# The two MLPs' down projections in another order: P6 with the middle products, P3 and P4 last, tile by tile

## The reference

```python
def sqrelu_mlp(x, w_up, w_down):
    return jnp.square(jax.nn.relu(x @ w_up)) @ w_down     # 1024 -> 4096 -> 1024

x = layer_norm(ALPHA * x + mix, ...)                      # attention, projected
x = layer_norm(ALPHA * x + sqrelu_mlp(x, mlp_w_up[layer], mlp_w_down[layer]), ...)
```

## Time and profile before

| | |
|---|---|
| time, median of 3 runs | 1939.84 us (1938.89 to 1945.38) |
| the profiled execution's own time | 1945.18 us |
| its span (first to last instruction) | 1943.4 us |
| PE busy | 1842.1 us (95%), 9436 matmuls |
| DVE busy | 1393.8 us (72%) |
| ACT busy | 882.3 us (45%) |
| POOL busy | 803.1 us (41%) |
| DMA | 297.86 MB, mean 153 GB/s |
| mean granted clock of PE | 0.979 |

### The profile page before, as it was taken

One profiled execution on the slowest core, in us unless ns is written; L12 is line 12 of the kernel. 1 busy time (PEld: TensorE's weight loads), 2 busy tenths in 40 slices (PEclk: granted clock), 3 DMA queues, 4 the chain that ended last, 5 costly groups with the idle time before them and its releaser, 6 DMA issues.

```text
span 1943.4 us, 25413 instructions
## 1 busy us (share of the span) xinstructions
PE 1842.1 (95%) x9436; PEld 1497.2 (77%) x9436; DVE 1393.8 (72%) x2217; ACT 882.3 (45%) x1512; POOL 803.1 (41%) x570
## 2 busy tenths in 40 slices
PE   9999899999999899999999999897999999999997
PEld 7877578777778788766877777677887888888876
DVE  4568857878898842275787888975559788776766
ACT  4247643444355432384343435465554554343442
POOL 1234533544451100182344444304446457777740
PEclk9999899999999899999999999898999999999999
DMA  7321033888866423203288886551211323333344
GB/s 282 109 91 45 1 141 97 318 295 288 293 234 197 151 87 108 88 2 98 96 316 282 293 291 246 178 174 45 87 66 47 128 84 112 109 109 130 109 152 152
DMA packets 66536, 297.86 MB, mean 153 GB/s; under 512 B 8496, under 2 KB 8816, under 8 KB 46064
## 3 DMA queue, kind: packets, MB, share of 16 engines
q1 hardware_dynamic: 59360, 254.45, 37.8%
q0 software_dynamic: 7056, 41.80, 5.9%
HBM read 258.54 MB, written 35.65 MB: 151 GB/s over the span
## 4 chain that ended last, share of the span: by engine, by line
PE 65%; DVE 21%; DMA 5%; ACT 3%; issue 3%; POOL 2%; SPq 0%; POOLq 0%; ACTq 0%; DVEq 0%
PE G L458 29%; PE G L2838 5%; PE G L2904 4%; PE TR L2904 4%; PE OB L2904 3%; DVE og_sb L3393 3%; DMA KS_sb<-ada 3%; DVE weights_low L666 2%; PE TR L458 2%; PE OB L458 2%; PE G L1906 2%; PE G L2857 2%; POOL weights_low L502 1%; PE TR L2838 1%; PE OB L1906 1%
## 5 line engine op out<-in xcount | busy, mean ns | idle before, releaser
L458 PE MATMUL G<-xt_high,weights_high 128*128 128x512 f32 (+1 forms) x1224 | 451.7, 369 | 0.7 <-DVE xt_low L1526 0.4
L458 PE MATMUL G<-xt_low,weights_high 128*128 128x512 f32 (+1 forms) x1224 | 449.7, 367 | 0.0
L458 PE MATMUL G<-xt_high,weights_low 128*128 128x512 f32 (+1 forms) x1224 | 449.5, 367 | 0.0
L502 POOL TENSOR_TENSOR weights_low<-ring_sb,weights_high 128x1024 fp32r<-128x1024 f32 (+2 forms) x102 | 244.4, 2408 | 300.4 <-ACT weights_high L496 300.4
L496 ACT ACTIVATE weights_high<-ring_sb 128x1024 fp32r<-128x1024 f32 (+2 forms) x188 | 189.6, 1019 | 158.4 <-DMA ring_sb<-chunks 43.6
L458 PEld LDWEIGHTS G<-xt_high,weights_high 128*128 128x128 f32 x1224 | 229.1, 187 | 41.0 <-issue 1.9
L458 PEld LDWEIGHTS G<-xt_high,weights_low 128*128 128x128 f32 x1224 | 228.9, 187 | 38.5
L458 PEld LDWEIGHTS G<-xt_low,weights_high 128*128 128x128 f32 x1224 | 228.9, 187 | 38.0
L666 DVE TENSOR_TENSOR weights_low<-ring_sb,weights_high 128x1024 fp32r<-128x1024 f32 (+1 forms) x160 | 200.8, 1258 | 78.6 <-ACT weights_high L659 78.2
L502 DVE TENSOR_TENSOR weights_low<-ring_sb,weights_high 128x1024 fp32r<-128x1024 f32 (+1 forms) x86 | 109.5, 1283 | 170.0 <-ACT weights_high L496 169.9
L659 ACT ACTIVATE weights_high<-ring_sb 128x1024 fp32r<-128x1024 f32 (+1 forms) x160 | 158.0, 989 | 117.9 <-PE G L2904 68.0
(11 more groups left out here) (637 smaller groups left out, 4288.8 us busy)
## 6 DMA issues: line engine op xcount, KB each, us to landing
ring_sb<-chunks SPq DMA_DIRECT2D x91, 1024.0 KB, 4.8
ring_sb<-ups SPq DMA_DIRECT2D x64, 512.0 KB, 4.1
KS_sb<-ada SPq DMA_DIRECT2D x64, 512.0 KB, 4.6
ring_sb<-down_sums SPq DMA_DIRECT2D x64, 512.0 KB, 3.9
ring_sb<-downs SPq DMA_DIRECT2D x16, 1024.0 KB, 6.9
down_sums<-ring_sb POOLq DMA_DIRECT2D x16, 1024.0 KB, 6.0
rows_sb<-downs SPq DMA_DIRECT2D x14, 1024.0 KB, 7.3
down_sums<-rows_sb POOLq DMA_DIRECT2D x14, 1024.0 KB, 5.9
```

The costliest lines, as they stand in the source:

```text
L458: mm = nc.tensor.matmul(out, lhsT=a, rhs=b, start=(3 * i + j == 0), stop=(3 * i + j == n - 1))
L502: tt_(out=quarter_part(wl, stage, n), in0=quarter_part(raw_quarter(stage, n), stage, n), in1=quarter_part(wh, stage, n), op=ALU.subtract). ...
```

## The change

The number of products, matmuls and split columns is the same. Their order and the engine of some of them differ.

- `LINEAR`: D14 now follows U31, D13 lies between U30 and U31, then B0, D15, B1 to B3. P6 leaves the last phase and becomes "S" (6 matmuls), interleaved with B from unit 3 on. The last phase is "C": P3 and P4 from one tile (12 matmuls per unit).
- `SPLITS`: ACT, DVE and SP follow their own list, which has C0 and C1 ahead of S15.
- `NORMAL` = 8 (first MLP) or 10 (second): from this unit on all C weights are held, and PE passes P3 tile 0, P3 tile 1, P4 tile 0, P4 tile 1, with a tile of the next stage transposed behind a pass.
- The buffer `KS4` now holds raw D14, not D15. B has three raw buffers instead of four, S two in XT.
- The modulation uses two buffers, `og` and `w2`; its PE sums stand one or two up products later; its part 1 ends behind D14.
- The low parts of C's staged hidden blocks (512 columns per unit) are made by POOL (`last_low`), no longer by DVE.
- In the second MLP POOL's `gpsimd_inputs` comes after all hidden sums, `scale_columns` behind C3, and the context's norm is cut in two, behind B8 and B11.

```diff
+    for u in range(11):
+        LINEAR += [("D", u), ("U", 6 + 2 * u), ("U", 7 + 2 * u)]
+    LINEAR += [("D", 11), ("U", 28), ("U", 29), ("D", 12), ("U", 30), ("D", 13), ("U", 31), ("D", 14), ("B", 0), ("D", 15)]
+    LINEAR += [("B", 1), ("B", 2), ("B", 3), ("S", 0)] + [x for u in range(4, 15) for x in (("B", u), ("S", u - 3))]
+    LINEAR += [("S", 12), ("B", 15), ("S", 13), ("S", 14), ("S", 15)] + [("C", u) for u in range(UNITS)]
-    ADA_SUM_BEHIND = {5: 0, 8: 1, 11: 2, 15: 3, 20: 4, 23: 5, 26: 6, 29: 7}
+    ADA_SUM_BEHIND = {7: 0, 10: 1, 13: 2, 16: 3, 21: 4, 25: 5, 28: 6, 31: 7}
+        ADA_SUM = [ogf, w2[:, :, :, :].rearrange("p a b c -> p (a b c)")]
...
         def raw_down(u):
-            return flat(KS4[:, :, :]) if u == UNITS - 1 else flat(rows[:, :, :]) if u % 2 else ring[:, 1, 2048:4096]
+            return flat(KS4[:, :, :]) if u == 14 else flat(rows[:, :, :]) if u % 2 and u < 15 else ring[:, 1, 2048:4096]
...
-                    elif u == UNITS - 1:
+                    elif u == 14:
                         sp.wait_ge(ada_steps, 64 * (i + 1))
+                    elif u == 15:
+                        sp.wait_ge(sums_stored[0], down_count(stage, 12))
...
+                def last_low(u):
+                    gp.wait_ge(staged_h, staged_at(stage, "C", u))
+                    tt(out=unit_r(u)[:, 1:3, :], in0=unit(u)[:, 1:3, :], in1=unit_r(u)[:, 0::3, :], op=ALU.subtract).then_inc(last_l, 1)
...
                 if stage == "mlp1":
-                    gpsimd_inputs(gp)
                 gain()
                 for u in range(UNITS):
-                    gp.wait_ge(staged_l, staged_at(stage, "B", u))
+                    gp.wait_ge(staged_l, low_at(stage, "B", u))
                     tt(out=a21, in0=a11, in1=a21, op=ALU.add).then_inc(hid_last, 1)
+                    if u >= 6:
+                        last_low(u - 6)
+                for u in range(UNITS - 6, UNITS):
+                    last_low(u)
+                if stage == "mlp1":
+                    gpsimd_inputs(gp)
...
+                normal = NORMAL[stage]
+                pe.wait_ge(dve_out, v + 14)
+                third(0, (0, 1))
+                for u in range(normal):
+                    if u + 1 < normal:
+                        third(u + 1, (0, 1))
+                    if u == 0:
+                        pe.wait_ge(dve_out, v + 18)
+                    fourth(u, (0, 1)).then_inc(quarters, 1)
+                for t in range(2):
+                    for u in range(normal, UNITS):
+                        mm = third(u, (t,), u == UNITS - 1)
+                    mm.then_inc(prod_done, 1)
+                    after(t)
+                for u in range(normal, UNITS):
+                    mm = fourth(u, (0,), u == UNITS - 1)
+                mm.then_inc(prod_done, 1)
+                after(2)
+                for u in LAST_PASS[stage]:
+                    fourth(u, (1,), u == LAST_PASS[stage][-1]).then_inc(quarters, 1)
+                after(3)
...
 # DVE, in mlp():
-                        if part or j:
-                            dve.wait_ge(ada_cols, 4 * part + j)
+                        if 4 * part + j > 1:
+                            dve.wait_ge(ada_cols, 4 * part + j - 1)
...
+                # behind the splits of all C tiles
+                quarters_in(dve, stage, AT["S", 15] + 1)
+                dve.wait_ge(dve_out, v + 18)
+                for t in range(2):
+                    evacuate(2 + t, 1, P6B[t])
+                    evacuate(2 + t, 0, P6B[t])
+                    evacuate(t, 1, P6B[t])
+                early(2, 1, 19)
+                early(3, 1, 22)
```

More of the change, by code:

```diff
@@ L661, in mlp_low, with mlp_weights @@
-        def mlp_low(dve, stage, n):
-            kind, u = LINEAR[n]
-            dve.wait_ge(w_hi, SPLIT0[stage] + n + 1)
-            wh, wl = mlp_weights(kind, u)
+                eng.wait_ge(first_sums_in[u % 3], 16 * ((6, 5, 5)[u % 3] * i + u // 3 + 1))
+            elif kind == "S":
+                eng.wait_ge(sixth_sums_in[u % 2], 16 * (8 * i + u // 2 + 1))
+            else:
+                eng.wait_ge(last_sums_in[u % 4], 32 * (4 * i + u // 4 + 1))
+        def mlp_weights(stage, kind, u):
+            if kind == "S":
+                return [x[:, 3, 512 * (u % 2):512 * (u % 2) + 512] for x in (Wh, Wl)]
+            if kind == "C" and u >= NORMAL[stage]:
+                row, last = HELD_IN[stage][u]
+                if row is not None:
+                    return flat(Hh[:, row:row + 2, :]), flat(Hh[:, row + 2:row + 4, :])
+                r = C_ROWS[last % 4]
+            else:
+                r = C_ROWS[u % 4] if kind == "C" else u % 3 if kind == "B" else 3 if (kind, u) == ("D", 15) else AT[kind, u] % 4
+            return Wh[:, r, :], Wl[:, r, :]
@@ L2978, in fourth, with last_left, third @@
+                def last_left(u, k):
+                    return [unit_r(u)[:, 3 * k, :], unit_r(u)[:, 1 + k, :]]
+                def third(u, ts, last=False):
+                    ready("C", "C", u)
+                    for t in ts:
+                        mm = block(P3B[t], t, last_left(u, 1), rights("C", u, 1), u == 0, last)
+                    return mm
+                def fourth(u, ts, last=False):
+                    ready("C", "C", u)
                     for t in ts:
-                        mm = block(P4B[t], t, lefts("A", u, 0), rights("F", u, 0), u == 0, u == UNITS - 1)
+                        mm = block(P4B[t], t, last_left(u, 0), rights("C", u, 0), u == 0, last)
@@ L3474, in evacuate, with early @@
                     ins.then_inc(dve_out, 1)
+                def early(t, half, n):
+                    dve.wait_ge(dve_out, v + n)
+                    nc.vector.bn_stats(stat[:, t, half, :], X[:, t, half * 512:(half + 1) * 512]).then_inc(ln_dve, 1)
                 done = 4
@@ new lines, in mlp, with last_tile @@
+                quarters_in(dve, stage, AT["S", 15] + 1)
+                dve.wait_ge(dve_out, v + 18)
+                for t in range(2):
+                    evacuate(2 + t, 1, P6B[t])
[3 more added lines that the diff above has]
+                early(3, 1, 22)
+                def last_tile(t, half):
+                    if t < 2:
+                        dve.wait_ge(prod_done, ends + 2 + t)
+                        dve.wait_ge(dve_out, v + (21, 24)[t])
+                        evacuate(t, 1, P3B[t])
+                    else:
@@ L3757, in _ @@
             xt_low_tile("x1", 0, 3)
-            mlp("mlp0", ALPHA, 0, lambda chain: {
-                ("bi", 0): lambda: chain(0), ("bi", 1): lambda: (chain(1), xt_low_tile("x2", 8, 0)), ("s1", 2): lambda: xt_low_tile("x2", 8, 1)})
+            mlp("mlp0", ALPHA, 0, between("x2", 8, True))
             xt_low_tile("x2", 8, 2)
```

521 lines of the change are left out of this document (240 added, 281 removed).

## The result

| | before | after |
|---|---|---|
| time, median, first comparison | 1940.8 us (1938.9 to 1945.4, 4 runs) | 1924.6 us (1923.4 to 1927.8, 4 runs) |
| time, median, a later comparison | 1945.7 us (1942.9 to 1947.6, 7 runs) | 1925.7 us (1924.1 to 1926.6, 4 runs) |
| the profiled execution's own time | 1945.2 us | 1925.5 us |
| its span | 1943.4 us | 1923.7 us |
| PE busy | 1842.1 us | 1835.0 us |

The ratio after to before is 0.9916 with a 95% interval of 0.9894 to 0.9938 in the first comparison and 0.9901 (0.9884 to 0.9917) in the later one: 16 and 19 us less. The forecast was 39 less, 1901 us. The time lies inside the range of 1880 to 1932, but the gain is half of what was forecast, or less.

The account below looks back on a forecast made before the run. PE was taken as the bound, busy for 95% of the span. 73.2 us go and 33.9 come, 39.3 less than the profiled 1945.2: 1905.9, as a median 1901 us; range 1880 to 1932.

Parts of the forecast that it names:

- what goes, all terms: Both MLPs: PE's idle and slow-clock time at modulation steps, D14, POOL's back-to-back sums and the MLP ends goes, 73.2 us.
- D13 behind raw D14: Between U30 and U31: PE newly waits 3.7 us for D13's hidden block, plus 1.6 of clock, twice: 10.6 us.
- D14 again: Behind U31: D14's block is late after B0's weight split, D15 and hidden sums; 3 us, twice: 6.
- the middle phase: Interleaved B and S units: DVE needs 4.7 us a unit against PE's 4.1; 2 and 5.5 us lost, sum 7.5.
- the tail: Last phase's tile 0: P6's evacuations behind C15's split make PE idle 2.0 and 4.1 us; with clock 9.8.
- nothing is relieved: Low parts on POOL (`last_low`): no relief for DVE, which waits while POOL works; no separate size given.
- the modulation: Up products: PE's ten waits for the last modulation step, 19.4 us, go, with 8 of clock: 27.4.
- the pile: Second MLP: POOL's ten back-to-back hidden sums after `scale_columns`, stalling DVE and PE, disappear; 10.2 us with clock.
- A: Rival: both new waits at D13 and D14 are absent because modulation runs ahead with two buffers; 1884 us, chance 0.20.
- B: Rival: up products are bound by loads, late modulation weights keep the 27.4 us of waits; 1928 us, chance 0.17.
- C: Rival: DVE and POOL hand-offs bound the middle phase, units 6 to 14, at 7.8 us each; 1960 us, chance 0.10.

## Why the prediction was wrong

By its own steps. The unit is idle time plus half of the slow-clock time. In the third column a slow stretch counts at half its length even where PE idled in it, so what came adds up to 57 and not to 54.7.

| step | forecast | in the trace after |
|---|---|---|
| what goes, all terms | 73.2 | 72.8 in the trace before |
| D13 behind raw D14 | 10.6 | 9.3 idle + 5.1 |
| D14 again | 6 | 4.3 + 1.7 |
| the middle phase | 7.5 | 12.2 idle + 5.1 |
| the tail | 9.8 | 7.0 idle + 7.1 (clock, and short waits) |
| short D and C waits | none | 5.3 |

- **The step that failed is "the middle phase"**, taken as 2 and 5.5 us. It summed DVE's work per unit (4.7 against PE's 4.1) and asked by how much nine units fall behind. In the trace a unit costs DVE 3.8 in the first MLP, and PE doesn't wait in these units but for 1.6 us in the second; the loss is one wait of 5.4 and 5.2 at the end, S15's, behind two splits and four evacuations. That was readable from the diff (`SPLITS` puts C0 and C1 ahead of S15) and wasn't priced. Shown: the order of these steps by itself is worth 8.2. The term is the largest miss, 9.8 of the 23 us by which what came was over the forecast; the others are 4.3 at the tail, 3.8 at D13, and 5.3 in short waits at D and C blocks that had no term.
- **The price of POOL's low part** is the second half of it. The prediction gave DVE's loss as 1.3 a unit and then took most of it as covered. In the units before the last it is covered, as staging four of them later shows. It isn't in front of S15, where C0's and C1's splits take 3.98 and not 2.4. Giving the work back to DVE is worth 9 to 10. The prediction's sentence that nothing is relieved was right, and it should have been a term of its own.
- **What goes was right in place, and wrong as a price.** All stalls named are absent after the change, but undoing the modulation costs 19.5, not 27.4, and undoing the pile 4.7, not 10.2, in either kernel. The modulation's waits came back in full, 19.9 us, and other waits shrank. As I read it, a stall that holds PE gives DVE time; when it goes, waits come elsewhere (1.8 and 1.6 at early D blocks; D13 and D14 together 10.6 with the modulation undone, 13.5 in the changed kernel).
- **D13** came where it was said, for the reason given: 4.3 and 5.0 of idle time where 3.7 was said; the clock cost 5.1 and not 3.2. But it wasn't a price either: taking it away moved it to D14, at 7.8, and removing both gave 4.7. D14's own wait came at the forecast's size, 6.0 in all.
- **The tail**'s two waits came as said (2.0 forecast and 2.8 measured; 4.1 and 4.1), but with clock and short waits it was 14.1 and not 9.8. Of these the first MLP's was shown to come from P6's late evacuations. In the second it was only in part.
- **Rivals.** A (no waits at D13 and D14) is refuted by the trace. B (late loads keep the modulation's waits) too: the DMA share stayed 0.82 and the waits are gone. C (DVE and POOL bound the middle phase, 1960) had the right engines and place, and far too high a price: POOL's low part lasts 1.48, not 3.1.

Left open: how much of the D13 and D14 loss is DVE's total work, since moving the three units' sums to freer units gave 2 us at most.

## What to carry to other kernels

When an engine is busy for 99% of a phase and another keeps just ahead of it, don't only compare their paces: look for the last unit before the pattern changes, and add up what stands in front of its last step. Price a removed stall by what is late next on the busiest helper, not by its length; here the two that were tested were worth 0.7 and 0.5 of their terms. And a buffer that frees the producer, and a place that frees the consumer, can each be worth nothing or less until both are there, so test them together before rejecting one.

## What the runs showed of the hardware

- A subtraction of 128x512 on POOL beside a busy DVE was a net loss: 0.8 us of standing in two kinds of DVE steps for 0.68 of work, and 9 to 10 us of the kernel's time for 32 of them. I had expected 8 at most. A sum of 128x256 broke even to within 3 us.
- POOL's own sum of 256 columns took 0.74 in the middle phase when the low parts were made by DVE, and 1.39 when POOL made them. With the pile put back, one DVE step of 512 columns took 4.97 us beside the last 3.2 us of seven such sums and the low part behind them:

```profile
1209.01 4.97 DVE L688 TENSOR_TENSOR weights_low<-XT_sb,weights_high 128x512 fp32r<-128x512 f32 x1
...
1207.34 4.87 POOL L2757 TENSOR_TENSOR wide_sb<-wide_sb 128x256 f32<-128x256 f32 x7
```

  It starts at 1209.0; POOL's sums end at 1212.2 and the low part at 1213.4, and the DVE step ends 0.5 later, at 1213.98. So a DVE step can stand behind several POOL steps in a row, not only the one that it met. The Trainium skill (SBUF, "two separate sides") speaks of a lock held for the whole instruction. I read that as letting DVE in after the first. The pile here and the one of the earlier trace rows, 7.60 beside ten sums in 6.84, show more than that; in the earlier trace rows the DVE step's row even begins 0.21 us ahead of POOL's first.
- DVE's steps with one operand in PSUM ran at 0.61 beside POOL's 128x1024 steps, those with both in SBUF stood (3.41 for 1.26).
